# Output projection of the attention layer cut by rows of head batches and issued between the last heads; modulation products of layer 1 inside the earlier batches

## The chip, the cores and the metric

The kernel runs on one core of one Trainium2 chip. The metric is the device time of one execution in microseconds (us). TensorE (PE) multiplies, VectorE (DVE) and ScalarE (ACT) read its results out of PSUM and do the elementwise work, GpSimd (POOL) does a little elementwise work from SBUF, and SyncE (SP) issues nearly all DMAs, in program order on one queue. Each engine works off its own list in order and waits on semaphores.

## The reference

Two layers over 256 tokens of width 1024. Layer 0 mixes tokens by causal pooling, layer 1 by dilated attention; each is followed by a mixture of 64 experts. Every sublayer is scaled, shifted and gated by a condition vector c:

```python
mod = silu(c) @ ada_w[i] + ada_b[i]            # sh1, sc1, g1, sh2, sc2, g2
hm  = x * (1 + sc1) + sh1
y   = dilated_attention_mixer(hm, w_in, w_out) # layer 1: 16 heads, 3 groups of keys,
                                               # mixed heads @ w_out at its end
x   = layer_norm(ALPHA * x + (1 + g1) * y)
hf  = x * (1 + sc2) + sh2
x   = layer_norm(ALPHA * x + (1 + g2) * moe(hf))
```

All of it is f32. The change touches `mixed @ w_out` of layer 1 and the order of the `silu(c) @ ada_w` products.

## The kernel before, in words

**Modulation.** `ada_w` of both layers is cut in 24 pieces of 1024x512 (2 MB each), numbered n = 0 to 23. `load_ada(n)` is SP's DMA. `ada(n)` on PE is 8 products with c, packed four abreast into one PSUM bank (`part_bank`); ACT rounds the result to f32r (`ada(n)` there), DVE puts the lower part beside it (`lower_rows`), and when the next piece comes, `flush()` on PE adds bias and parts with two matmuls into bank 6 + n % 2 (`BSUM`), which ACT copies to `modb`. Pieces 12 to 23 belong to layer 1: 16 to 19 shift and scale of its expert sublayer, 20 and 21 the gate of attention, 22 and 23 the gate of the experts. Before the change 12 to 16 are done ahead of attention, 17 to 21 inside it (`ada_of_head`: 17, 18, 19 in batches 0, 1, 2, and 20 and 21 in the last), 22 and 23 behind it.

**Attention.** Keys, queries and values are projected from h in slices: slice n is 1 MB of `attn_w_in`, for a batch `hb` of four such heads, nine slices a batch; PSUM bank 6 + n % 2. Products are f32 by three f32r matmuls (`three`: high by high, low by high, high by low). So each slice is cast by ACT (`slice_high`, line 760) and its rest taken by DVE (`slice_low`, line 421) into one of two buffers `wr`. SP loads slice n into one of four units as soon as slice n - 4 has been lowered (`w_lo`), with the `load_ada`s written in between.
There are 16 heads of 64 columns; what the code counts as a head h, and this text too, is a pair of them for one tile of 128 of the queries, again 16 in all (`place`). For each: `scores(h)` on PE (line 1419), `head_scores` on DVE (bias, line 1088, and maximum, line 1093), exponential (line 792) and division (line 796) on ACT, eight transposes on PE (line 1443) to banks 2 and 3, copies to `pT` by ACT and DVE (lines 802, 1111), the product with the values on PE (line 1456) to bank 4, and DVE's copy to `mixedT` (line 1120), which signals `o_ready`. While the heads of batch hb run, the slices of batch hb + 1 are projected between them (`proj_of_head`: two per head, three in the last head of a batch). In the last batch nothing is left to project. There ACT and DVE also cast the mixed heads of the batches that are done (`mixed_high`, line 782, `mixed_low`, line 1099).

**Output projection.** Slices 36 to 39 are four column blocks of 256 of `attn_w_out`, each with all 1024 rows. A block needs all sixteen heads, so the four come after head 15: 192 matmuls of 256 columns. Slices 38 and 39 are cast while 36 and 37 are multiplied. Then PE does ada(22) and ada(23), and `norm(2)` on DVE and ACT adds, gates and normalizes (`residual`, lines 884 to 895; `deviation`; ACT's line 701), token tile 0 then 1; `modulate` makes h for the experts (POOL tile 0, DVE tile 1, lines 403 and 405). `moe(1)` begins with PE transposes (line 1182) and the router (line 1248), and its loop over 32 pairs of experts follows.
SP, behind head 15: the shared expert's weights, ada piece 22 once slice 39 is lowered, and the experts once `y_ready` and `ada_mm` 24 are there.

Of the kernel before, what the change touches and what calls it, by code (L numbers as in the profile page):

```python
# [131 lines left out]
def build(nc, a, out):  # L132
    ctx = ExitStack()
    with ctx:
# [118 lines left out]
        ada_unit = [0, 2, 4, 6, 4, 0, 2, 4, 0, 2, 6, 4, 0, 2, 6, 4, 9, 9, 9, 9, 9, 9, 2, 0]  # L253
# [5 lines left out]
        def part_bank(n):  # L259

            return 5 if n % 2 == 0 or 16 <= n < 22 else (3 if n == 15 else 4)
# [105 lines left out]
        def ada_of_head(hb, hh):  # L367

            return {(0, 1): 17, (1, 1): 18, (2, 1): 19, (3, 0): 20, (3, 2): 21}.get((hb, hh))
# [55 lines left out]
        def _(sp):  # L425
# [90 lines left out]

            def load_slice(n):
                if n < 9 * BATCHES:
                    src = a["attn_w_in"][n % 9, n // 9]
                else:  # L520
                    src = a["attn_w_out"][n - 9 * BATCHES]
                sp.dma_start(units(n % RAW, 1), src).then_inc(raw_in[n % RAW], 16)
# [9 lines left out]
            for n in range(RAW, SLICES):  # L532
                if n in (RAW, 20, 29, 38):
                    m = 17 + (RAW, 20, 29, 38).index(n)
                    sp.wait_ge(ada_mm, m)
                    load_ada(m)
                sp.wait_ge(w_lo, n - RAW + 1)
                load_slice(n)
            sp.wait_ge(ada_mm, 21)
            load_ada(21)  # L540
            sp.wait_ge(w_lo, SLICES - 2)
            load_ada(23)
            sp.wait_ge(ada_mm, 22)
            sp.wait_ge(o_ready, HEADS)
            shared(1)
            sp.wait_ge(w_lo, SLICES)
            load_ada(22)
            sp.wait_ge(y_ready, 3 * TT)
            sp.wait_ge(ada_mm, 24)
# [85 lines left out]
        def _(act):  # L635
# [150 lines left out]
            for hb in range(BATCHES):  # L786
                for hh in range(HB):
                    h = hb * HB + hh
                    before, after = proj_of_head(hb, hh)
                    for j in range(2):  # L790
                        act.wait_ge(max_ready, 2 * h + j + 1)
                        nc.scalar.activation(sp_[:, j], sp_[:, j], ACT.Exp, bias=negmax[:, j:j + 1],
                                             accum_out=zsum[:, j:j + 1]).then_inc(p_exp, 1)
# [9 lines left out]
                    if hb == BATCHES - 1 and hh < HB - 1:  # L803
                        mixed_high(hh)
                    for n in after:
                        projected(n)
            flush()
            act.wait_ge(o_ready, HEADS)
            mixed_high(BATCHES - 1)
            slice_high(SLICES - 2)  # L810
            slice_high(SLICES - 1)
            ada(22)
            norm(2, (0,))
            ada(23)
            norm(2, (1,))
            flush()
# [5 lines left out]
        def _(dve):  # L822
# [57 lines left out]
            def residual(n, t):  # L880

                gate = G1 if n % 2 == 0 else G2
                dve.wait_ge(y_ready, TT * n + t + 1)
                V.tensor_tensor(PS[:, 2 * t:2 * t + 2, :], PS[:, 2 * t:2 * t + 2, :],
                                modb[:, gate].rearrange("p (b n) -> p b n", b=2), ALU.mult).then_inc(y_read, 1)
                dve.wait_ge(y_read, TT * n + t + 1)
                step(V.scalar_tensor_tensor(tmp[:, t], x[:, t], ALPHA, PS[:, 2 * t:2 * t + 2, :].rearrange("p b n -> p (b n)"),
                                            ALU.mult, ALU.add))
# [14 lines left out]
            def norm(n):  # L903
# [6 lines left out]
                if n == 2:  # L910
                    lower_rows(22)
# [9 lines left out]
                if n == 2:  # L921
                    lower_rows(23)
# [179 lines left out]
            for h in range(HEADS):  # L1102
# [17 lines left out]
                last = copy(in_order(mixedT, 2 * hb + pair)[:, 2 * it:2 * it + 2], PS[:, 4, 0:P].rearrange("p (r i) -> p r i", r=2))  # L1120
# [3 lines left out]
                if hb == BATCHES - 1:  # L1124
                    mixed_low(hh)
                elif hh == HB - 1:
                    head_scores(h + 1)
            for n in (SLICES - 2, SLICES - 1):
                slice_low(n)
# [11 lines left out]
        def _(pe):  # L1141
# [259 lines left out]

            for n in range(9):
# [21 lines left out]
            for hb in range(BATCHES):  # L1424
                for hh in range(HB):
# [9 lines left out]
                    if n is not None and before:  # L1435
                        ada(n)
                    if h:
                        pe.wait_ge(pT_act, h)
                        pe.wait_ge(pT_dve, h)
                    for j in range(2):  # L1440
# [8 lines left out]
                    if h:  # L1449
                        pe.wait_ge(o_ready, h)  # L1450
                    _, pair, it = place(h)
                    for c in range(4):
                        for j in range(2):
                            col = (0, 1, it, it)[c] * BCOL + (2 * pair + j) * HD
                            v = qkv[:, hb % 2, (0, 0, 1, 2)[c], 2, col:col + HD]
                            last = mm(PS[j * HD:(j + 1) * HD, 4, 0:P], v, pT[:, j, c * P:(c + 1) * P], start=c == 0, stop=c == 3,  # L1456
# [5 lines left out]
            pe.wait_ge(hT_act, 12)  # L1462
            pe.wait_ge(hT_dve, 12)
            for n in range(SLICES - 4, SLICES):
                q = n - (SLICES - 4)
                pe.wait_ge(w_lo, n + 1)
                w = wr[:, n % 2]
                for t in range(TT):
                    for k in range(KD):
                        def parts(ph, pw):  # L1470
                            return (hThi, hTlo)[ph][:, k, t * P:(t + 1) * P], w[:, pw, k, :]
                        last = three(PS[:, 2 * t + q // 2, (q % 2) * BCOL:(q % 2 + 1) * BCOL], parts, k == 0, k == KD - 1)
                    if q == 3:
                        last.then_inc(y_ready, 1)
                if q < 3:
                    last.then_inc(proj_mm, 1)
            for n in (22, 23):
                ada(n)
            flush()
# [7 lines left out]
def packed(v):  # L1487
# [16 lines left out]
    v["attn_w_out"] = k_p(v["attn_w_out"][0], BCOL)  # L1504
# [21 lines left out]
```

## Time and profile before

| | us |
|---|---|
| median of 3 runs | 1578.89 |
| lowest, highest | 1572.59, 1582.16 |
| the profiled execution | 1582.94 |
| its span, first to last instruction | 1581.2 |

The profile is of one execution. Its times are us from the span's start. In a timeline a row is: start, duration, engine, line and operation, output and inputs, how many; in brackets the idle time of the engine just before and what ended it. In the chain of waits a row is: start, duration, what the end of the program hung on in that time. A row of a stretch gives the busy time of each engine with the number of instructions, then the granted TensorE clock (1.00 is 2.4 GHz, 0.50 is 1.2 GHz), the share of the DMA engines, and GB/s.

### The profile page before, as it was taken

Reading aid. Unit: us, or ns where it says so; the run is one execution under the profiler, and the core shown is the slowest. Engines: PE = TensorE matmul, PEld = TensorE weight load, DVE = VectorE, ACT = ScalarE, POOL = GpSimd, SP = SyncE. Lnnn points to the kernel's source line nnn. Section 1 sums busy time; section 2 is a strip of 40 time slices with the busy share of each in tenths; the row PEclk is TensorE's granted clock in tenths of the full one; section 3 lists DMA queues with packets and bytes.
Section 4 is the critical chain, followed back from the end, with each engine's and each line's share of the span. In section 5 each row is a group of like instructions: output and inputs, shape, how many; then the busy total and the mean of one; then the engine's idle time right before and its main releaser. Section 6 shows DMA issues by size and latency. Waiting matters only on the chain.

```text
span 1581.2 us, 19822 instructions
## 1 busy us (share of the span) xinstructions
PE 1477.7 (93%) x7858; PEld 873.9 (55%) x7858; DVE 500.6 (32%) x966; ACT 400.0 (25%) x633; POOL 98.6 (6%) x77
## 2 busy tenths in 40 slices
PE   4998999999999999959999997879999999999995
PEld 1454555455455454449899995745454454454552
DVE  2115222222222222254545545451222222222224
ACT  1123111121121111234545554231111111111112
POOL 1003022000000000051000000030200000000001
PEclk8998999999999999979999997879999999999997
DMA  9786599999999999555353543356999999999990
GB/s 377 317 363 288 239 398 423 426 427 425 427 427 423 424 424 423 233 228 201 131 206 109 211 183 137 141 240 250 419 426 423 428 426 425 425 424 425 420 393 27
DMA packets 50042, 520.23 MB, mean 329 GB/s; under 512 B 5752, under 2 KB 6008, under 8 KB 7880
## 3 DMA queue, kind: packets, MB, share of 16 engines
q1 hardware_dynamic: 48584, 514.73, 78.8%
q0 software_dynamic: 1408, 4.79, 0.9%
q8 instruction: 37, 0.61, 0.1%
q14 instruction: 13, 0.11, 0.0%
HBM read 518.44 MB, written 1.05 MB: 329 GB/s over the span
## 4 chain that ended last, share of the span: by engine, by line
PE 89%; DVE 5%; ACT 2%; DMA 2%; issue 1%; SPq 0%; DVEq 0%; ACTq 0%
PE psum L1336 28%; PE psum L1361 15%; PE psum L1292 8%; PE psum L1283 8%; PE psum L1380 5%; PE psum L1381 5%; PE psum L1382 5%; PE psum L1171 2%; DMA weights<-in_ada_w 2%; PE psum L1202 2%; PE psum L1256 2%; PE psum L1232 2%; PE psum L1443 1%; PE psum L1456 1%; PE psum L1274 1%
## 5 line engine op out<-in xcount | busy, mean ns | idle before, releaser
L1336 PE MATMUL psum<-weights,slots_of_tokens 128*64 128x512 f32 x2048 | 452.2, 592 | 0.0
L1336 PEld LDWEIGHTS psum<-weights,slots_of_tokens 128*64 128x64 f32 x2048 | 175.8, 137 | 263.8 <-issue 263.8
L1361 PE MATMUL psum<-weights,hidden_T 128*64 128x512 f32 x1024 | 233.8, 597 | 4.3
L1047 DVE SCALAR_TENSOR_TENSOR slot_rows<-psum,slot_weight,slot_rows 128x512 fp32r<-128x512 f32 x128 | 96.1, 751 | 243.7 <-ACT slot_rows L745 243.7
L1361 PEld LDWEIGHTS psum<-weights,hidden_T 128*64 128x64 f32 x1024 | 80.9, 136 | 128.5 <-issue 128.5
L1033 DVE TENSOR_TENSOR hidden<-gate,psum 128x256 f32<-128x256 f32 x64 | 27.0, 423 | 372.4 <-ACT gate L737 372.4
L1292 PE MATMUL psum<-slot_rows,slots_T 128*128 128x512 f32 x528 | 140.1, 407 | 3.7 <-DVE slot_rows L1047 3.7
L1283 PE MATMUL psum<-slot_matrix,h_parts 128*128 128x512 f32 x512 | 141.9, 399 | 0.0
L1292 PEld LDWEIGHTS psum<-slot_rows,slots_T 128*128 128x128 f32 x528 | 94.2, 188 | 74.5 <-issue 57.3
L737 ACT ACTIVATE gate<-psum 128x256 f32<-128x256 f32 x64 | 24.7, 386 | 409.7 <-PE psum L1336 409.7
L745 ACT ACTIVATE slot_rows<-psum,slot_weight 128x512 fp32r<-128x512 f32 x128 | 88.1, 689 | 156.6 <-PE psum L1361 156.6
L1380 PE MATMUL psum<-h_transposed_high,slice_parts 128*128 128x256 f32 x384 | 110.1, 287 | 5.2 <-DVE slice_parts L421 3.3
L421 DVE TENSOR_TENSOR slice_parts<-weights,slice_parts 128x2048 fp32r<-128x2048 f32 x38 | 88.9, 2347 | 69.1 <-ACT slice_parts L760 69.1
L1381 PE MATMUL psum<-h_transposed_low,slice_parts 128*128 128x256 f32 x384 | 108.6, 283 | 0.0
L1382 PE MATMUL psum<-h_transposed_high,slice_parts 128*128 128x256 f32 x384 | 108.6, 283 | 0.0
L1283 PEld LDWEIGHTS psum<-slot_matrix,h_parts 128*128 128x128 f32 x512 | 91.5, 189 | 16.8
L1035 DVE COPY slots_of_tokens<-psum 128x512 f32<-128x512 f32 x64 | 44.2, 691 | 136.2 <-PE psum L1283 136.2
L760 ACT CAST slice_parts<-weights 128x2048 fp32r<-128x2048 f32 x40 | 75.8, 1895 | 12.6 <-PE psum L1382 12.1
L1380 PEld LDWEIGHTS psum<-h_transposed_high,slice_parts 128*128 128x128 f32 x384 | 73.5, 192 | 8.3 <-issue 7.3
L1380 PE MATMUL psum<-slice_parts,h_transposed_high 128*128 128x256 f32 x256 | 74.0, 289 | 2.0 <-ACT h_transposed_high L782 2.0
L1381 PEld LDWEIGHTS psum<-h_transposed_low,slice_parts 128*128 128x128 f32 x384 | 73.6, 192 | 0.0
L1382 PEld LDWEIGHTS psum<-h_transposed_high,slice_parts 128*128 128x128 f32 x384 | 73.6, 192 | 0.0
(179 smaller groups left out, 1452.3 us busy)
## 6 DMA issues: line engine op xcount, KB each, us to landing
weights<-in_exp_w_gu SPq DMA_DIRECT2D x128, 2048.0 KB, 13.5
weights<-in_exp_w_down SPq DMA_DIRECT2D x128, 1024.0 KB, 11.6
weights<-in_ada_w SPq DMA_DIRECT2D x24, 2048.0 KB, 10.9
weights<-in_attn_w_in SPq DMA_DIRECT2D x36, 1024.0 KB, 4.8
weights<-in_pool_w_in SPq DMA_DIRECT2D x2, 2048.0 KB, 31.4
weights<-in_pool_w_out SPq DMA_DIRECT2D x1, 4096.0 KB, 13.2
weights<-in_sh_w_gu SPq DMA_DIRECT2D x2, 2048.0 KB, 10.8
weights<-in_attn_w_out SPq DMA_DIRECT2D x4, 1024.0 KB, 4.8
```

The costliest lines, as they stand in the source:

```text
L421: ops.tensor_tensor(wr[:, n % 2, 1], slice_w(n), wr[:, n % 2, 0].bitcast(F32), ALU.subtract).then_inc(w_lo, 1)
L745: nc.scalar.activation(yw[:, 0, half * HALF:(half + 1) * HALF], PS[:, BD + half, :], ACT.Copy, scale=wslot[:, 0:1]).then_inc(lo.yh, 1)
L760: copy(wr[:, n % 2, 0], slice_w(n)).then_inc(w_hi, 1)
L1035: copy(XgT[1 - i // 4][:, 2 * (i % 4), :], PS[:, BG, :]).then_inc(lo.copy_dve, 1)
L1047: V.scalar_tensor_tensor(yw[:, 1, c], PS[:, BD + half, :], wslot[:, 0:1], yw[:, 0, c].bitcast(F32), ALU.mult, ALU.subtract).then_inc(lo.yl, 1)
L1283: last = mm(PS[:, bank, :], hfs[:, s, t, k, :], Pm[b][:, t, :], start=s == 0 and t == 0, stop=s == 1 and t == TT - 1)
L1292: last = mm(PS[:, 2 * t + half, :], PT[:, t * P:(t + 1) * P], yw[:, s, half * HALF:(half + 1) * HALF], start=False, stop=True, skip_group_ ...
L1336: last = mm(PS[j * SLOTS:(j + 1) * SLOTS, BGU, :], XgT[ob][:, k, s0:s0 + SLOTS], gu_w(ws + j)[:, k, :], start=k == 0, stop=k == KD - 1, ti ...
L1361: last = mm(PS[j * SLOTS:(j + 1) * SLOTS, BD + half, :], HT[:, k, j * SLOTS:(j + 1) * SLOTS], dn_w(ws + j)[:, k, half * HALF:(half + 1) * ...
L1380: mm(out, *parts(0, 0), start=first, stop=False)
L1381: mm(out, *parts(1, 0), start=False, stop=False)
L1382: return mm(out, *parts(0, 1), start=False, stop=last)
```

## The change

Four things are changed together.

1. `attn_w_out` is cut by rows: slice 36 + q holds the 256 rows of `mixed` that head batch q produces, with all 1024 columns. `out_project(q)` multiplies them: 2 token tiles x 2 column halves x 2 row blocks x 3 = 24 matmuls of 512 columns, summed over q in PSUM (`mixer_bank`: banks 6, 7 for tile 0, banks 4, 5 for tile 1). q = 0, 1, 2 stand ahead of the transposes of heads 13, 14, 15; q = 3 behind head 15. `residual` reads the new banks.
2. ada pieces 17 to 23 all stand in batches 0 to 2 (PE, ACT and DVE), in partial bank 5; SP's loads of them move to `ADA_AT`. ACT and PE flush piece 23 at head 13.
3. The product with the values goes to bank 2 in place of 4, so PE now waits for the copy of head h - 1 (`o_ready`) ahead of the transposes of head h, not ahead of its value product.
4. `slice_high`/`slice_low` of 38 and 39 move into heads 13 and 14.

```diff
-        ada_unit = [0, 2, 4, 6, 4, 0, 2, 4, 0, 2, 6, 4, 0, 2, 6, 4, 9, 9, 9, 9, 9, 9, 2, 0]
+        ada_unit = [0, 2, 4, 6, 4, 0, 2, 4, 0, 2, 6, 4, 0, 2, 6, 4, 9, 9, 9, 9, 9, 9, 9, 9]
...
-            return {(0, 1): 17, (1, 1): 18, (2, 1): 19, (3, 0): 20, (3, 2): 21}.get((hb, hh))
+            return {(0, 1): 17, (0, 3): 18, (1, 1): 19, (1, 2): 20, (1, 3): 21, (2, 1): 22, (2, 3): 23}.get((hb, hh))
+        def mixer_bank(t):
+            return 6 - 2 * t
...
+            ADA_AT = (RAW, 15, 19, 23, 26, 28, 33)
-                if n in (RAW, 20, 29, 38):
-                    m = 17 + (RAW, 20, 29, 38).index(n)
+                if n in ADA_AT:
+                    m = 17 + ADA_AT.index(n)
                     sp.wait_ge(ada_mm, m)
                     load_ada(m)
                 sp.wait_ge(w_lo, n - RAW + 1)
                 load_slice(n)
-            sp.wait_ge(ada_mm, 21)
-            load_ada(21)
-            sp.wait_ge(w_lo, SLICES - 2)
-            load_ada(23)
-            sp.wait_ge(ada_mm, 22)
             sp.wait_ge(o_ready, HEADS)
             shared(1)
-            sp.wait_ge(w_lo, SLICES)
-            load_ada(22)
             sp.wait_ge(y_ready, 3 * TT)
-            sp.wait_ge(ada_mm, 24)
             experts(1)
...
+                    if h == HEADS - HB + 1:
+                        flush()
...
                     if hb == BATCHES - 1 and hh < HB - 1:
                         mixed_high(hh)
+                        if hh:
+                            slice_high(9 * BATCHES + hh + 1)
...
-            flush()
             act.wait_ge(o_ready, HEADS)
             mixed_high(BATCHES - 1)
-            slice_high(SLICES - 2)
-            slice_high(SLICES - 1)
-            ada(22)
-            norm(2, (0,))
-            ada(23)
-            norm(2, (1,))
-            flush()
+            norm(2)
...
-                last = copy(in_order(mixedT, 2 * hb + pair)[:, 2 * it:2 * it + 2], PS[:, 4, 0:P].rearrange("p (r i) -> p r i", r=2))
+                last = copy(in_order(mixedT, 2 * hb + pair)[:, 2 * it:2 * it + 2], PS[:, 2, 0:P].rearrange("p (r i) -> p r i", r=2))
...
                 if hb == BATCHES - 1:
                     mixed_low(hh)
+                    if hh in (1, 2):
+                        slice_low(9 * BATCHES + hh + 1)
...
-            for n in (SLICES - 2, SLICES - 1):
-                slice_low(n)
...
+            def out_project(q):
+                n = 9 * BATCHES + q
+                pe.wait_ge(w_lo, n + 1)
+                pe.wait_ge(hT_act, 8 + q + 1)
+                pe.wait_ge(hT_dve, 8 + q + 1)
+                w = wr[:, n % 2].rearrange("p w k n -> p w (k n)").rearrange("p w (k n) -> p w k n", k=2)
+                for t in range(TT):
+                    for half in range(2):
+                        for k in range(2):
+                            def parts(ph, pw):
+                                return (hThi, hTlo)[ph][:, 2 * q + k, t * P:(t + 1) * P], w[:, pw, k, half * HALF:(half + 1) * HALF]
+                            last = three(PS[:, mixer_bank(t) + half, :], parts, q == 0 and k == 0, q == BATCHES - 1 and k == 1)
+                    if q == BATCHES - 1:
+                        last.then_inc(y_ready, 1)
+                if q < BATCHES - 1:
+                    last.then_inc(proj_mm, 1)
...
+                    if hb == BATCHES - 1 and hh:
+                        if hh == 1:
+                            flush()
+                            pe.wait_ge(ada_mod, 24)
+                            pe.wait_ge(proj_copied, 9 * BATCHES)
+                        out_project(hh - 1)
                     if h:
                         pe.wait_ge(pT_act, h)
                         pe.wait_ge(pT_dve, h)
+                        pe.wait_ge(o_ready, h)
...
-                    if h:
-                        pe.wait_ge(o_ready, h)
...
-            for n in range(SLICES - 4, SLICES):
-                q = n - (SLICES - 4)
-                pe.wait_ge(w_lo, n + 1)
-                w = wr[:, n % 2]
-                for t in range(TT):
-                    for k in range(KD):
-                        def parts(ph, pw):
-                            return (hThi, hTlo)[ph][:, k, t * P:(t + 1) * P], w[:, pw, k, :]
-                        last = three(PS[:, 2 * t + q // 2, (q % 2) * BCOL:(q % 2 + 1) * BCOL], parts, k == 0, k == KD - 1)
-                    if q == 3:
-                        last.then_inc(y_ready, 1)
-                if q < 3:
-                    last.then_inc(proj_mm, 1)
-            for n in (22, 23):
-                ada(n)
-            flush()
+            out_project(BATCHES - 1)
             moe(1)
...
-    v["attn_w_out"] = k_p(v["attn_w_out"][0], BCOL)
+    v["attn_w_out"] = v["attn_w_out"][0].reshape(BATCHES, 2, P, D).transpose(0, 2, 1, 3).reshape(BATCHES, P, UNIT)
```

## Rows read from the trace of the kernel before

**Rows 1.** Page of the profile, busy time over the span: us, share, instructions.

```profile
PE 1477.7 (93%) x7858; PEld 873.9 (55%) x7858; DVE 500.6 (32%) x966; ACT 400.0 (25%) x633; POOL 98.6 (6%) x77
```

**Rows 2.** Busy time by stretch: inside the batches, and heads 14 and 15.

```profile
780.00:840.00 60.00, 58.37 (x520) 56.34 (x520) 33.51 (x46) 30.26 (x41) 0.00 (x0) 1.00 0.47 176
...
985.00:997.00 12.00, 6.33 (x49) 5.13 (x48) 6.04 (x15) 4.55 (x9) 0.00 (x0) 0.66 0.01 1
```

**Rows 3.** Timeline of PE, value products of heads 4 to 6 and ada between.

```profile
835.40 1.09 PE L1456 MATMUL psum<-probabilities_T,qkv 128*64 128x128 f32 x16
...
847.31 0.35 PE L1380 MATMUL psum<-h_transposed_high,slice_parts 128*128 128x256 f32 x1 [0.40 <-issue]
...
853.22 1.09 PE L1456 MATMUL psum<-probabilities_T,qkv 128*64 128x128 f32 x16
...
868.04 1.09 PE L1456 MATMUL psum<-probabilities_T,qkv 128*64 128x128 f32 x16
```

**Rows 4.** DMA issues between 690 and 1000 us: count, KB each, median us to landing.

```profile
weights<-in_ada_w SPq DMA_DIRECT2D x6, 2048.0 KB, 9.9
```

**Rows 5.** Chain of waits, heads 12 to 15.

```profile
967.65 1.95 PE psum L1443 x8
...
970.32 1.46 DVE scores L1088 x6
971.81 1.28 DVE negative_maximum L1093 x2
...
974.04 0.52 DVE h_transposed_low L1099
...
975.53 1.95 PE psum L1443 x8
...
991.74 1.96 PE psum L1443 x8
```

**Rows 6.** Timeline of PE, scores of head 14.

```profile
972.33 2.08 PE L1419 MATMUL psum<-qkv 64*128 64x256 f32 x12
```

**Rows 7.** Chain of waits, from the end of head 15 to the router.

```profile
996.49 0.73 PE psum L1159
...
998.27 0.52 ACT h_transposed_high L782
...
1000.16 0.21 PE psum L1381
...
1002.84 0.12 PE psum L1382
...
1012.77 1.92 ACT slice_parts L760
1014.71 2.30 DVE slice_parts L421
1017.03 7.69 DMA weights<-in_ada_w
...
1043.60 7.06 PE psum L1248 x32
```

**Rows 8.** Timeline of DVE, same stretch: fold, residual of tiles 0 and 1, modulation.

```profile
1016.92 0.68 DVE L393 TENSOR_TENSOR folded_shift<-norm_gain_bias,modulation 128x512 f32<-128x512 f32 x1
...
1021.45 1.23 DVE L884 TENSOR_TENSOR psum<-psum,modulation 128x1024 f32<-128x1024 f32 x1 [0.34 <-PE psum L1382]
...
1029.82 1.23 DVE L884 TENSOR_TENSOR psum<-psum,modulation 128x1024 f32<-128x1024 f32 x1
...
1038.03 1.23 DVE L405 TENSOR_TENSOR residual_or_h<-residual_or_h,modulation 128x1024 f32<-128x1024 f32 x1
```

**Rows 9.** Timeline of DVE, the norm between the layers: residual of tiles 0 and 1.

```profile
675.36 1.23 DVE L884 TENSOR_TENSOR psum<-psum,modulation 128x1024 f32<-128x1024 f32 x1 [0.37 <-DVE slot_of_token L1053]
...
680.15 1.23 DVE L884 TENSOR_TENSOR psum<-psum,modulation 128x1024 f32<-128x1024 f32 x1
```

**Rows 10.** Chain of waits in the expert loop: four f32r matmuls of 512 columns.

```profile
1090.39 0.93 PE psum L1283 x4
```

More of the change, by code:

```diff
@@ L259, in part_bank @@
         def part_bank(n):
-            return 5 if n % 2 == 0 or 16 <= n < 22 else (3 if n == 15 else 4)
+            return 5 if n % 2 == 0 or 16 <= n else (3 if n == 15 else 4)
         def ada_w(n):
@@ L882, in residual @@
                 gate = G1 if n % 2 == 0 else G2
+                b0 = mixer_bank(t) if n == 2 else 2 * t
+                y = PS[:, b0:b0 + 2, :]
                 dve.wait_ge(y_ready, TT * n + t + 1)
-                V.tensor_tensor(PS[:, 2 * t:2 * t + 2, :], PS[:, 2 * t:2 * t + 2, :],
-                                modb[:, gate].rearrange("p (b n) -> p b n", b=2), ALU.mult).then_inc(y_read, 1)
+                V.tensor_tensor(y, y, modb[:, gate].rearrange("p (b n) -> p b n", b=2), ALU.mult).then_inc(y_read, 1)
                 dve.wait_ge(y_read, TT * n + t + 1)
-                step(V.scalar_tensor_tensor(tmp[:, t], x[:, t], ALPHA, PS[:, 2 * t:2 * t + 2, :].rearrange("p b n -> p (b n)"),
-                                            ALU.mult, ALU.add))
+                step(V.scalar_tensor_tensor(tmp[:, t], x[:, t], ALPHA, y.rearrange("p b n -> p (b n)"), ALU.mult, ALU.add))
                 step.settle()
@@ L909, in norm @@
                 deviation(n, 0)
-                if n == 2:
-                    lower_rows(22)
                 if n == 0:
@@ L920, in norm @@
                     lower_rows(12)
-                if n == 2:
-                    lower_rows(23)
             def route(L):
@@ L1455, in _ @@
                             v = qkv[:, hb % 2, (0, 0, 1, 2)[c], 2, col:col + HD]
-                            last = mm(PS[j * HD:(j + 1) * HD, 4, 0:P], v, pT[:, j, c * P:(c + 1) * P], start=c == 0, stop=c == 3,
+                            last = mm(PS[j * HD:(j + 1) * HD, 2, 0:P], v, pT[:, j, c * P:(c + 1) * P], start=c == 0, stop=c == 3,
                                       tile_position=(0, j * HD))
@@ L1461, in _ @@
             flush()
-            pe.wait_ge(hT_act, 12)
-            pe.wait_ge(hT_dve, 12)
-            for n in range(SLICES - 4, SLICES):
-                q = n - (SLICES - 4)
-                pe.wait_ge(w_lo, n + 1)
-                w = wr[:, n % 2]
-                for t in range(TT):
-                    for k in range(KD):
-                        def parts(ph, pw):
-                            return (hThi, hTlo)[ph][:, k, t * P:(t + 1) * P], w[:, pw, k, :]
-                        last = three(PS[:, 2 * t + q // 2, (q % 2) * BCOL:(q % 2 + 1) * BCOL], parts, k == 0, k == KD - 1)
-                    if q == 3:
-                        last.then_inc(y_ready, 1)
-                if q < 3:
-                    last.then_inc(proj_mm, 1)
-            for n in (22, 23):
-                ada(n)
-            flush()
+            out_project(BATCHES - 1)
             moe(1)
```

## Prediction

> **What bounds the kernel now.** Look first at the page's busy times: PE is busy for 93% of the span [rows 1], so what counts is work added to or taken from PE, and the few places where PE stands idle. The busy times by stretch show where these are. Inside the batches PE works 58.4 of 60 us at 2.4 GHz, and the other engines half of that: each instruction added there is paid in full. In the last batch, with no slice left to project, PE works 6.3 of 12 us at a mean granted clock of 0.66 [rows 2]: there a chain of short steps through DVE, ACT and PE sets the time, so PE has room, but DVE and ACT have little. The chain of waits then shows the third place, the tail behind head 15: from the last value product (its end is where the first row of [rows 7] begins, 996.49) to the end of the modulation that lets PE transpose for the experts (1038.03 + 1.23 = 1039.26 [rows 8]) it takes **42.8 us**. The 192 matmuls of the projection, a DMA of piece 22 that holds the chain for 7.69 us once slice 39 is lowered [rows 7], ada(22) and ada(23) and the norm lie on it. The router follows at 1043.60 [rows 7]. From there on the change touches nothing, so I price three stretches: batches, last heads, tail.
>
> **Batches: four more ada.** Three ada stand in batches 0 to 2 before, seven after. Value product to value product, head 5 with an ada takes 853.22 - 835.40 = 17.82 us, head 6 with as many projections and none takes 14.82: an ada costs 3.0 us, of which 0.4 is PE waiting for ACT to free the sum's bank for the next projection of that parity [rows 3]. That wait comes only where the sum's number has the parity of the next slice: for 17, 18 and 19 before, for 17, 18, 20 and 21 after. So the four add 4 x 2.6 + 0.4 = **+10.8 us**. Nothing hides that, since PE is full [rows 2]. Their ACT and DVE parts (two copies, one subtraction, under 2 us a piece) fit beside engines that are half idle there. DMA: `load_ada` is now ahead of the slice load in six places and waits for the ada before it. An ada piece lands after 9.9 us [rows 4], and the slice queued behind it soon after, since the pair is moved together; I take 10 to 11 us from the end of the ada. The tightest places are slices 19 and 28, behind the ada of a batch's last head: their cast could begin when transposes and one more slice are done, 1.0 + 5.8 + ACT's copy 0.6, with the 0.4 and the sum's matmuls 0.6, 8.4 us after the ada. So the cast (1.92) comes 1.6 to 2.6 us late; DVE meanwhile is at the value copy and the lower part of the slice before, 2.30 [rows 7], so 0 to 1.5 us come through at each of two places; I take 0. If the landing were still later, head scores of the next batch would wait behind that slice on DVE, and the head's transposes on PE for them. The new wait for `o_ready` ahead of the transposes stands behind a whole slice of projection, 48 matmuls at 0.12 [rows 7] or 5.8 us, in which DVE only needs its copy: free here.
>
> **Last heads.** I lay out time from the start of head 12's transposes (967.65). Before: heads 13 and 15 begin their transposes at 7.88 and 24.09 [rows 5], and head 15's value product ends at 28.84 [rows 7]. The same chain after the change:
> - Head 12: transposes 1.95 and copy to 2.7, bias to 4.15, maxima to 5.4 [rows 5]. PE's value product ends at 4.75 (as 991.74 to 996.49 for head 15 [rows 5, 7]), scores of head 14 take 2.08 [rows 6], to 6.8. Now the new wait: ACT stands at `flush()` ahead of head 13's exponential until PE has done the two sum matmuls (0.73 + 0.44), then copies for 0.6, so piece 23 is in `modb` at 8.65 (the same three steps run from 996.49 to 998.27 [rows 7]). Only then come exponential, reciprocal and division for head 13, about 2.6 us; they end near 11.3, still beside out_project(0).
> - **out_project**: 24 matmuls of 512 columns. Four cost 0.93 at 2.4 GHz [rows 10], so 5.6 us. At 1.2 GHz a matmul of 256 columns takes 0.21 against 0.12 [rows 7], so one of 512 about 0.43 (an estimate from these), 10.3 us for all 24. PE has been working for some 6 us when q = 0 starts at 8.7, and in the tail of before the clock rose 3 us after the first projection matmul, near 1002.7 [rows 7]; so I give q = 0 6.5 us. Head 13's transposes begin at 15.2, not 7.88.
> - Heads 14 and 15: the period is transposes 1.0 (half of the 1.95 at the low clock), copy 0.75, bias 1.46, maxima 1.28 [rows 5], value copy 0.3 (part of the 0.95 between the end of head 13's maxima and the start of its lower part; ada's `lower_rows`, now gone from there, is the rest), `mixed_low` 0.52 [rows 5], signals 0.15, out_project 5.6: 11.1 us. out_project must wait for `mixed_low` of the same batch of channels, which stands behind `head_scores` on DVE; that wait is the new link. The casts of slices 38 and 39 (ACT 1.92, DVE 2.30 us [rows 7]) delay the reciprocal, and so put division's end at 8.8 us of the period, 2.3 us ahead of out_project's end: hidden now, but only by it. Before, the three periods were 7.88, and 16.21 for two [rows 5], with ada(21) in the path of one.
> - Between value product and out_project(2) PE idles 2.4 us, as no scores are left. I take the clock as falling there and add 1.5 us (7 matmuls at the low price). Nearest row: [rows 2] for 985 to 997, at 0.66.
> So head 15's transposes begin at 15.2 + 11.1 + 11.1 + 1.5 = 38.9, and its value product ends 3.0 later, at 42.0, not 28.84: **+13.2 us**. Bounds: +11.7 with the clock high throughout; each out_project at the low clock would add 4.7, so +25 at worst.
>
> A rule of the Trainium skill bears on this. The rows show the last heads at 0.66 of full clock [rows 2], with eight transposes at 1.95 us [rows 5]. The page "TensorE: Matmul & The Clock Gate", section "HAM oscillation — how this bites in real kernels", says that bursts of matmuls between waits keep falling back to the low clock and pay the ramp each time, and its Part 4 says that transposes do not count as busy. By that rule each of the three projections between heads would start low, as in my second rival; by the rows the clock had risen to full within the tail of before.
>
> **Tail.** From the end of head 15's value product: DVE's copy 0.5 with its signal, then cast on ACT, lower part on DVE and PE's start, 1.4 us (998.27 for the cast, and the projection's matmul at 1000.16 is its third, 0.4 to 0.5 us behind the first [rows 7]): PE starts at 1.95, DVE is free at 1.85. Tile 0 takes 12 matmuls: 2.8 us at the high clock, 5.2 at the low, 4.2 with a rise on the way, so `y_ready` comes at 6.2. DVE needs 1016.92 to 1021.11 = 4.2 us for `fold_norm` [rows 8], which used to lie beside the projection; it ends at 6.05. Residual of tile 0 starts at 6.25. Without ada(22) in ACT's way the second tile's starts 4.8 us later, as in the norm between the layers [rows 9] (before: 8.4, from 1021.45 to 1029.82 [rows 8]). From there to the end of the modulation it took 9.44 us (1029.82 to 1039.26 [rows 8]), which I keep, since `lower_rows`, which goes, stood in the shadow of ACT. Sum 6.25 + 4.8 + 9.4 = 20.5, against 42.8: **-22.3 us**. With `y_ready` at the extremes (4.8 with fold in front, 7.2) it is -22.5 to -21.3. Next in line behind it are ACT's two casts for the experts, then the router 4.3 us after the modulation, as before [rows 7, 8]. The loads of router and shared weights start at the end of head 15 in both; the router's has 24.8 us in place of 47.1 (20.5 or 42.8, and 4.3), and 0.25 MB lands well within that beside 3 MB of shared weights, by the 9.9 us of a 2 MB piece [rows 4]. The experts' loads still start ahead of the router.
>
> **Sum.** +10.8 + 13.2 - 22.3 = **+1.7 us**: the span 1581.2 becomes 1582.9, the execution 1582.94 becomes 1584.6. That execution lies 4.05 above the median of the runs, 1578.89, so the median after should be **1580.6 us**. The work taken from the tail is nearly all still paid: the 23 us of projection matmuls are issued between heads whose chain they lengthen, and ada 22 and 23, with 20 and 21 which lay in idle time, go where PE is full.
>
> **Rivals.**
> - *Faster, the projection fits the gaps.* If the products slip beside DVE's and ACT's work, the heads keep their old 8 us periods plus the flush, +3 in place of +13.2: total -8.5, 1570.4. For it: PE is idle half of that stretch [rows 2]. Against it: program order puts out_project between scores and transposes, and it waits for `mixed_low`, so it cannot use the idle time before. It decides if out_project starts before the maxima end.
> - *Slower, the clock stays low between heads.* Every out_project at the low price: 3 x 4.7 less the 2.4 already counted, and 1 us for tile 0 in the tail, +13: total +14.5, 1593.4. It decides if the rows of out_project lie 0.43 us apart beyond the first 3 us. For it: 0.66 in [rows 2], and the skill's rule. Against: PE will be busy 9 of 11 us per head.
> - *Slower, slices late.* The loads behind `load_ada` block ACT and through it DVE: if the pairs land 3 us later than I take, two boundaries and one head pay about 2 us each, +6: 1586.6.
> - *The overlap isn't there.* If something keeps q = 1 and 2 behind head 15 (a flush, `w_lo` 39), two pieces of 5.6 return to the tail, and the heads lose 2 x 3; total +7, 1585.9.
>
> **How the numbers follow.** Forecast, between -3 and +5 around the sum: 0.58. Fits the gaps or is otherwise clearly faster: 0.17. Clock: 0.10. Slices late: 0.09. No overlap: 0.06. The runs of before spread by 0.6%, so a 1% change, 15.8 us, is about what can be told from none. Faster by over 1% would need the first rival and the ada hidden as well: 0.05. Slower by over 1% is the clock rival with some slices late: 0.07. The range takes the first rival and most of the clock rival: 1569 to 1593.
>
> **What would show it.** Heads 5 and others with an ada again at 17.8, and 7 of them. In heads 14 and 15 a period near 11, with DVE's `h_transposed_low` (line 1099 before) as what releases the first matmul of out_project; exponential of head 13 released by ACT's own `modulation` copy. The tail from last value product to the modulation's end at 20 to 21 us, with no DMA in the chain. Wrong if the period is 8 to 9 or above 13, if granted clock in the last heads stays under 0.7, or if PE waits at the start of a batch for a slice's lower part more than it does now.

## The result, and the profile after

The changed kernel takes **1581.62 us** (median of 20 runs, 1576.69 to 1589.05) against 1578.03 us for the kernel before (20 runs, 1572.59 to 1585.31): ratio 1.003, 95% interval 1.0018 to 1.0041. That is 3.6 us slower in the medians, forecast were 1.7, a change of 0.3%, far below the 2% from which one calls a kernel slower. Its profiled execution took 1582.43 us and has a span of 1580.7 us.

To see where time went I cut each trace at five points that both kernels have: the start of head 0's value product, the start of head 12's transposes, the end of head 15's value product, the end of `modulate` of tile 1, and the first matmul of the expert loop. Each number is a difference of row starts or ends in the timelines of PE and DVE, in us; "to expert loop" runs from the end of `modulate` to the first matmul of the loop:

| profile | batches | last heads | tail | to expert loop | sum |
|---|---|---|---|---|---|
| before | 201.8 | 28.8 | 42.8 | 42.0 | 315.4 |
| before, second | 201.9 | 26.5 | 43.1 | 42.7 | 314.1 |
| before, third | 201.8 | 28.8 | 42.7 | 42.0 | 315.3 |
| changed | 215.5 | 40.8 | 20.9 | 37.1 | 314.2 |
| changed, second | 215.3 | 41.0 | 21.3 | 37.1 | 314.6 |
| changed, third | 215.1 | 40.8 | 20.9 | 37.1 | 313.9 |
| e1 slices first | 212.4 | 40.8 | 20.9 | 37.1 | 311.1 |
| e2 ada only | 215.5 | 26.5 | 40.9 | 42.4 | 325.2 |
| e3 project behind | 215.3 | 30.0 | 35.3 | 37.1 | 317.6 |
| e4 flush at 12 | 215.4 | 40.5 | 22.4 | 40.1 | 318.4 |
| e5 ada at 12 | 212.6 | 40.4 | 20.8 | 40.4 | 314.3 |
| e6 transposes first | 215.2 | 33.9 | 20.9 | 42.2 | 312.2 |
| e7 combined | 209.8 | 32.1 | 20.9 | 37.1 | 299.9 |

Changed against before: **+13.7, +12.0, -21.9, -4.9**. The first three are the forecast's +10.8, +13.2 and -22.3. The fourth was not forecast. Head 0's value product itself starts anywhere from 761.2 to 766.4 us in these six profiles of the two kernels, so some 5 us of difference between executions arise ahead of everything that the change touches.

**Batches.** The timeline of PE in the changed kernel, value products of heads 4 and 5, the ada of head 6, and a slice:

```profile
840.00 1.09 PE L1470 MATMUL psum<-probabilities_T,qkv 128*64 128x128 f32 x16
...
857.18 1.09 PE L1470 MATMUL psum<-probabilities_T,qkv 128*64 128x128 f32 x16
...
865.23 1.92 PE L1162 MATMUL psum<-weights,condition_repeated 128*32 128x512 f32 x16
...
870.26 0.36 PE L1371 MATMUL psum<-slice_parts,h_transposed_high 128*128 128x256 f32 x1 [1.58 <-issue]
```

Head 5 now takes 857.18 - 840.00 = 17.18 us against 17.82 in [rows 3]: the wait of 0.4 is absent, as the prediction's rule of parity says (it comes only where the number of the sum and of the next slice are both even or both odd, and so share a bank). The other 0.24 means that an ada without the wait costs 2.4 us here and not 2.6. But in head 6 PE waits 1.58 us where 0.4 was due. ACT's timeline (the idle time before each cast, and its releaser) shows why:

```profile
824.09 1.90 ACT L758 CAST slice_parts<-weights 128x2048 fp32r<-128x2048 f32 x1 [1.87 <-DMA weights<-in_attn_w_in]
...
861.23 1.91 ACT L758 CAST slice_parts<-weights 128x2048 fp32r<-128x2048 f32 x1 [3.35 <-DMA weights<-in_attn_w_in]
...
901.37 1.90 ACT L758 CAST slice_parts<-weights 128x2048 fp32r<-128x2048 f32 x1 [1.97 <-DMA weights<-in_attn_w_in]
```

Slices 19, 23 and 28 come late. SP had issued their ada pieces at 813.72, 850.03 and 890.90; the casts start 10.4, 11.2 and 10.5 us later. Behind slices 19 and 28 PE waits at the first transposes of the next batch, 0.77 and 0.87 us, for ACT's division.

**Last heads.** Chain of waits of the changed kernel (start, duration, what the end hung on):

```profile
981.83 1.95 PE psum L1459 x8
...
986.62 2.01 PE psum L1428 x12
988.63 0.72 PE psum L1150
989.35 0.32 PE psum L1151
989.70 0.60 ACT modulation L648
990.35 0.50 PE psum L1371
...
996.11 0.89 PE psum L1459 x8
...
999.19 1.28 DVE negative_maximum L1084 x2
...
1000.77 0.53 DVE h_transposed_low L1090
...
1001.43 0.47 PE psum L1371
...
1012.49 0.47 PE psum L1371
...
1013.43 0.43 PE psum L1371
...
1017.06 0.23 PE psum L1371
...
1019.81 0.89 PE psum L1459 x8
```

Read it against [rows 5]: head 13's transposes no longer wait for ACT's division but stand behind out_project(0), which stands behind scores, the two sum matmuls (lines 1150, 1151) and ACT's copy of the sum (line 648). In heads 14 and 15 `mixed_low` (line 1090) releases out_project (line 1371), and out_project releases the transposes. The period is 11.05 us, then 12.65. In out_project(2) the first three matmuls lie 0.23 to 0.31 us apart, the next eight 0.40 to 0.43, the rest 0.23: the clock fell just behind its start, not ahead of it. Granted clock by stretch:

```profile
985.00:997.00 12.00, 11.29 (x62) 8.69 (x58) 3.21 (x10) 3.34 (x7) 0.00 (x0) 0.82 0.00 1
997.00:1009.00 12.00, 8.93 (x62) 7.27 (x64) 7.43 (x15) 6.68 (x11) 0.00 (x0) 1.00 0.00 0
1009.00:1020.00 11.00, 8.52 (x44) 6.80 (x45) 5.57 (x12) 4.82 (x8) 0.00 (x0) 0.84 0.01 2
```

PE is busy 28.7 of 35 us, at 0.82 to 1.00, where [rows 2] had 6.3 of 12 at 0.66.

**Tail.** Chain of waits and, last, the router: fold's first step, residual of tile 0 and of tile 1, the modulation's end, transposes, router.

```profile
1024.37 0.70 DVE folded_shift L397
...
1028.64 1.25 DVE psum L881
...
1033.51 1.16 DVE psum L881
...
1042.28 1.24 DVE residual_or_h L409
1043.56 3.47 PE psum L1173 x15
...
1047.86 3.76 PE psum L1239 x32
```

No DMA and no ada is left there. DVE's fold of 4.2 us, which lay beside the projection in [rows 8], now decides when the residual starts. The router takes 3.76 us, not the 7.06 of [rows 7]: it is at the high clock from its first matmul. That is where the 4.9 us of the last stretch come from (3.3 here, the rest in the matmuls behind it). Granted clock of the changed kernel in the 15 transposes and in the router, then of the kernel before in the router:

```profile
1043.56:1047.03 3.47, 3.47 (x15) 3.06 (x15) 0.69 (x1) 3.40 (x4) 3.40 (x3) 0.50 0.97 413
1047.86:1051.61 3.75, 3.75 (x33) 3.75 (x34) 0.00 (x0) 0.24 (x1) 3.44 (x2) 1.00 1.04 446
```

```profile
1043.60:1050.66 7.06, 7.06 (x33) 7.06 (x34) 0.00 (x0) 0.68 (x1) 3.45 (x2) 0.50 1.00 427
```

In the changed kernel the clock rises between the transposes and the router; in the kernel before, with the same transposes ahead of the router, it is low to the router's end.

### The profile page after: what moved, and what is told of

Its sections match the earlier page's. It is cut to its first block, busy times and chain, and to the rows that moved or that the text cites. A ratio compares the mean times of both kernels' runs of the same rounds, so it can differ in the third digit from the quotient of the medians.

```text
span 1580.7 us, 19647 instructions
## 1 busy us (share of the span) xinstructions
PE 1467.6 (93%) x7762; PEld 861.8 (55%) x7762; DVE 501.0 (32%) x966; ACT 399.4 (25%) x633; POOL 98.2 (6%) x77
## 4 chain that ended last, share of the span: by engine, by line
PE 88%; DVE 6%; DMA 3%; ACT 2%; issue 1%; SPq 0%; DVEq 0%; ACTq 0%
PE psum L1327 28%; PE psum L1352 15%; PE psum L1283 8%; PE psum L1274 8%; PE psum L1371 4%; PE psum L1372 4%; PE psum L1373 4%; PE psum L1162 2%; PE psum L1193 2%; PE psum L1247 2%; PE psum L1223 2%; DMA weights<-in_ada_w 1%; DMA weights<-in_attn_w_in 1%; PE psum L1265 1%; PE psum L1459 1%
## 5 line engine op out<-in xcount | busy, mean ns | idle before, releaser
L1371 PE MATMUL psum<-slice_parts,h_transposed_high 128*128 128x256 f32 (+1 forms) x224 | 68.6, 306 | 8.6 <-DVE h_transposed_low L1090 5.5
## 6 DMA issues: line engine op xcount, KB each, us to landing
weights<-in_exp_w_down SPq DMA_DIRECT2D x128, 1024.0 KB, 11.2
weights<-in_sh_w_gu SPq DMA_DIRECT2D x2, 2048.0 KB, 10.8
```

The source lines that it names most:

```text
L1371: mm(out, *parts(0, 0), start=first, stop=False)
```

## The experiments

e1 to e4 ran on one chip, e5 to e8 on another; each was also timed against the kernel before. The changed kernel itself ran beside e5 to e8 only. Stretches are those of the one profiled execution of each, and executions of one kernel differ by several us, so the medians of 5 to 12 runs are given too.

**e1_slices_first.** Are the 2.9 us that the batches cost above the forecast the late slices?

```diff
-            ADA_AT = (RAW, 15, 19, 23, 26, 28, 33)
+            ADA_AT = (RAW, 16, 20, 24, 27, 29, 34)
```

> The changed kernel, with each of SP's loads of an ada piece issued one slice later, so that slices 15, 19, 23, 26, 28 and 33 go ahead of the piece and no longer wait for the ada before it. Theory (slices late): ACT's casts no longer wait for a DMA (7.7 us in the changed kernel), the three heads behind slices 19, 23 and 28 lose 0.9, 1.2 and 1.0 us, and the four extra ada cost 10.8 us as forecast, not 13.7: 3 us less than the changed kernel, ratio to the kernel before about 1.001. Rival (the waits are covered, the extra is something else, such as ACT's or DVE's queue): casts start earlier and the stretch from head 0's value product to head 12's transposes stays at 215.5 us.

Measured: batches 212.4, 3.1 less than changed, all else equal to 0.1 us; 1578.67 us, ratio 1.0005 (0.9996 to 1.0013). Group of ACT's casts from 780 us to head 12, first in the changed kernel, then in e1 (count | busy, mean | idle before, releaser):

```profile
L758 ACT CAST slice_parts<-weights 128x2048 fp32r<-128x2048 f32 x24 | 45.5, 1894 | 7.2 <-DMA weights<-in_attn_w_in 7.2
```

```profile
L758 ACT CAST slice_parts<-weights 128x2048 fp32r<-128x2048 f32 x24 | 45.4, 1891 | 0.0
```

The waits for a DMA are gone and with them the 3 us; the rival falls. What is left of the batches' cost, 212.4 - 201.8 = 10.6 us, is the forecast's 10.8 for four ada.

**e2_ada_only.** What does the move of the ada pieces do by itself?

```diff
 # the kernel before, with only:
-        ... 9, 9, 9, 9, 9, 9, 2, 0]
+        ... 9, 9, 9, 9, 9, 9, 9, 9]
-            return {(0, 1): 17, (1, 1): 18, (2, 1): 19, (3, 0): 20, (3, 2): 21}.get((hb, hh))
+            return {(0, 1): 17, (0, 3): 18, (1, 1): 19, (1, 2): 20, (1, 3): 21, (2, 1): 22, (2, 3): 23}.get((hb, hh))
 # SP's loads and waits and the partial bank as in the change; ada(22), ada(23) and their parts gone from the tail
```

> The kernel before with part 2 of the change alone: ada pieces 17 to 23 in batches 0 to 2, SP's loads as in the change; projection in column blocks behind head 15 and value product in bank 4 as before. Theory: the batches cost +13.7 us as in the changed kernel, the last heads lose ada 20 and 21 (-1.3), the tail loses only what ada 22 and 23 held up beyond the projection (42.8 to about 39.2): +8.8 us against before, ratio 1.0055. Rival (the two ada of the tail and the DMA ahead of them were the main cost there): the tail shrinks by 10 us or more and the kernel is level with before or faster.

Measured: batches +13.7, heads -2.4, tail -1.9, together +9.4 of the expected +8.8; 1592.35 us, ratio 1.0068 (1.0047 to 1.009). Two of its nine runs took 1580.2 and 1580.6, at a granted clock of 0.968 against 0.961 to 0.964 in the others; no profile shows one of them. The 2.4 us of the heads cannot be put down to ada 20 and 21: the second profile of the kernel before has the same 26.5 with both in place. The tail's chain in e2: the projection's first and last matmul, the residual.

```profile
1011.26 0.55 PE psum L1364
...
1033.90 0.13 PE psum L1366
1034.16 1.24 DVE psum L872
```

With the two ada and their DMA gone the tail still takes 40.9 us, since the projection lies on it from 1011.26 to 1034.03. The rival, a tail 10 us shorter, falls: the ada of the tail were nearly free there, the four more in the batches are not.

**e3_project_behind.** Is it worth anything to issue the products between heads?

```diff
-                        out_project(hh - 1)
...
-            out_project(BATCHES - 1)
+            for q in range(BATCHES):
+                out_project(q)
 # slice_high / slice_low of 38 and 39 behind head 15's casts
```

> The changed kernel with all four products by rows issued behind head 15 (slices 38 and 39 cast there too), the rest as changed. Theory (the products between heads cost 12 us there, but save some 17 us of the tail and the clock's ramp): heads 13 to 15 go back to periods near 8 us, from head 12's transposes to head 15's last value product 32 us instead of 40.8, the tail goes from 20.9 to 38.4: +8.7 us against the changed kernel, ratio to before 1.008. Rival (moving them is worth nothing, all is paid between the heads): within 2 us of the changed kernel, 1.003.

Measured: heads 30.0, tail 35.3, 3.5 us more than changed in both together (expected 8.7; the rival allowed 2). Median 1584.88, ratio 1.0032 (1.0017 to 1.0048). Chain of waits: transposes of heads 13, 14, 15, the last cast, the fold, the residual.

```profile
992.27 1.91 PE psum L1458 x8
...
999.72 1.19 PE psum L1458 x8
...
1006.45 1.96 PE psum L1458 x8
...
1023.19 1.92 ACT slice_parts L758
...
1027.35 0.70 DVE folded_shift L397
...
1031.62 1.24 DVE psum L881
```

Without the products between them heads 14 and 15 come in 7.45 and 6.73 us. So the three products lengthen the heads by 10.8 us (40.8 - 30.0) and shorten the tail by 14.4 (35.3 - 20.9). About three quarters of what is saved behind is paid in front. Neither theory's number was right; the truth lay between them. The three products take 17.2 us of the tail (1011.17 to 1028.38), and it grows by only 14.4: the first of them starts at once, while out_project(3) of the changed kernel waits 1.94 us for `mixed_low`, and DVE's fold ends 1.1 us behind out_project(3)'s first tile there and 0.3 us in e3.

**e4_flush_12.** Is the sum of piece 23 in head 13 a cost of its own?

```diff
 # ACT and PE
-                    if h == HEADS - HB + 1:          (PE: if hh == 1, ahead of out_project)
+                    if h == HEADS - HB:              (PE: ahead of scores(h + 1))
                         flush()
```

> The changed kernel with the sum of piece 23 at head 12, where PE and ACT stand idle, and not at head 13. Theory (the flush is a wait of its own in head 13): out_project(0) starts right behind the scores of head 14, 1.7 us earlier, and the exponential of head 13 3.5 us earlier; the heads are 1.7 us shorter, ratio to before 1.002. Rival (head 13 is bound by mixed_low and the clock's rise, so the flush is hidden): under 0.5 us.

Measured: out_project(0) starts right behind the scores, and head 13's transposes come 12.7 us behind head 12's, not 14.1. But heads and tail together are 62.8 us, 1.2 more than changed, and the median is 1584.82, ratio 1.0038 (1.0025 to 1.0051). Chain of waits, out_project(2), out_project(3) and the residual:

```profile
1010.15 0.77 PE psum L1371
...
1015.61 0.39 PE psum L1371
...
1023.29 0.76 PE psum L1371
...
1028.89 1.24 DVE psum L881
```

The 1.4 us are there and are lost again: out_project(2) now runs its first 13 matmuls at the low clock, and out_project(3) its first 14, with them its whole first tile, 5.5 us, so that `y_ready` is late where DVE's fold had covered it. The step that I expected happened, its worth did not arrive. That the earlier product is what moved the clock is argued from one profile: in the second profile of the changed kernel out_project(3) starts with six matmuls at the low clock too, and the intervals of the two kernels overlap.

**e5_ada_12.** Does an ada cost its price only where PE is full?

```diff
-... (2, 1): 22, (2, 3): 23}.get((hb, hh))
+... (2, 1): 22, (3, 0): 23}.get((hb, hh))
```

> The changed kernel with ada piece 23 at head 12, where PE idles 5.7 us, in place of batch 2. Theory (an ada costs its 2.6 to 3.0 us only where PE is full): from head 0's value product to head 12's transposes 2.6 us less, heads the same within 0.3, ratio 1.001. Rival (the price of an ada in the batches comes from ACT and DVE): less than 1 us saved, or given back in head 13, whose sum waits for the lower rows: ratio 1.003.

Measured: batches 212.6, 2.9 us less, heads 0.4 less: the theory's 2.6 to 3.0. Its last stretch was 40.4 against 37.1 us, as the clock fell again inside the router (4.75 us); median 1581.47, ratio 1.0022 (1.0006 to 1.0038), which cannot be told from the 1581.57 of the changed kernel beside it.

**e6_transposes_first.** Is the 11 us period order, or work?

```diff
 # PE: out_project from ahead of the transposes to behind them; flush at head 12
                     last.then_inc(t_mm, 1)
+                    if hb == BATCHES - 1 and hh:
+                        ...
+                        out_project(hh - 1)
 # DVE, last batch
+                if hb == BATCHES - 1:
+                    if hh >= 2:
+                        slice_low(9 * BATCHES + hh)
+                    if hh < HB - 1:
+                        inverse(h + 1)            # the reciprocal, ahead of the value copy
                 dve.wait_ge(o_mm, h + 1)
 # ACT: slice_high(9 * BATCHES + hh) behind the pT copies of heads 14 and 15
```

> The changed kernel with out_project(q) between the transposes and the value product of its head, the reciprocal of the next head ahead of DVE's copy, slices 38 and 39 cast one head later, and the sum of piece 23 at head 12. Theory (the period of 11.1 us is PE's out_project waiting for mixed_low, with the transposes behind it): PE's own work, 1.0 + 5.6 + 1.1 + 1.1, sets a period near 9, from head 12's transposes to the last value product 33.5 to 35 us instead of 40.8, at least 6 us off, ratio 0.999. Rival (DVE's and ACT's queues bind, with the casts): periods stay at 10.5 or more, 1 us off at most, ratio 1.002.

Measured: heads 33.9 us, 6.9 less; 1579.33 us, ratio 0.9996 (0.9979 to 1.0013), 2.2 us less than the changed kernel beside it. The rest went at the router: it ran at the low clock, and the last stretch took 42.2 us, 5.1 more. Chain of waits:

```profile
986.01 1.94 PE psum L1463 x8
987.95 0.43 PE psum L1379
...
996.64 1.04 PE psum L1463 x8
...
1001.16 2.20 DVE slice_parts L425
1003.36 0.09 DVE softmax_inverse L1095
...
1004.86 1.07 PE psum L1463 x8
```

Head 15 comes 8.3 us behind head 14, head 14 10.6 behind 13, as out_project(0) still starts with six matmuls at the low clock. What ends the shorter period is again a cast: slice 38's lower part (line 425) holds the reciprocal. The rival falls: one period is above its 10.5, but for the clock, and it allowed 1 us off in all. The sum of piece 23 at head 12 is in this kernel too, worth 1.4 us to head 13 in e4; the other moves of e6 were not tried one by one.

**e7_combined.** e1, e5 and e6 together, the sum of piece 23 behind head 14's scores.

> Slices ahead of the ada pieces, piece 23 at head 12 with its sum behind the scores of head 14, and transposes ahead of out_project, all in the changed kernel. Theory: the parts add, batches -3.1 - 2.6, heads -6.7, tail unchanged: 12 us less than the changed kernel in the stretches up to the router, ratio to the kernel before 0.995, and 0.998 at worst where the clock is low. Rival (what is taken out returns as time at the low clock): under half of it, ratio 0.999 or more.

Measured: batches -5.7 (expected -5.7), heads -8.7 (-6.7), tail equal, 14.4 us less than changed up to the router; 1572.04 us (1562.55 to 1576.28), ratio to before **0.9957** (0.9939 to 0.9975). In the medians it is 9.5 us faster than the changed kernel beside it and 6.4 faster than the kernel before, and the rival (0.999 or more) falls. But the profiled execution, 1562.68 us at a granted clock of 0.975, is one of two such; the ten others took 1570.3 to 1576.3 at 0.965 to 0.968, and no profile shows where their 7.6 us or more go. So the 14.4 us are this kernel at its best. In that execution the clock is at full from 978.5 us to past the last head:

```profile
971.00:978.50 7.50, 6.27 (x38) 4.87 (x39) 5.04 (x13) 4.94 (x11) 0.00 (x0) 0.60 0.01 2
978.50:990.00 11.50, 11.48 (x76) 9.42 (x77) 6.04 (x17) 6.50 (x13) 0.00 (x0) 1.00 0.00 0
990.00:1003.00 13.00, 12.30 (x82) 9.82 (x80) 8.02 (x11) 6.59 (x9) 0.00 (x0) 1.00 0.01 2
```

**e8_changed_again, e9_before_again, e10_before_third, e11_changed_third.** Both kernels unaltered, more profiles, to see which differences are of the kernel and which of the execution.

> The changed kernel, unaltered, on the same chip as the kernels beside it. Theory (between head 12 and the experts PE's clock falls and rises at places that differ from execution to execution): the stretches of the batches come out as before within 0.5 us (215.5), while heads, tail and router stage differ by up to 5 us from the first profile's 40.8, 20.9 and 37.1 us. Rival (the clock's course is the kernel's own): all four stretches the same within 0.3 us. Ratio 1.003 in both.

> The kernel before, unaltered, one more profile. Theory (the stage from the end of the modulation to the expert loop falls at 37 or at 42 us with PE's clock, in either kernel, from execution to execution): one of the two profiles of the kernel before in this call has it at 37 to 40, so that the 4.9 us by which the changed kernel's first profile was shorter there is no effect of the change. Rival (the longer wait ahead of the router in the kernel before fixes the clock's course): 42.0 within 0.3 in both, and 37.1 in the changed kernel.

> The kernel before, unaltered, a third profile; theory and rival as for the second: 37 to 40 us in one of the two, or 42.0 in both, from modulation to expert loop. Batches 201.8, heads 28.8, tail 42.8 us within 0.5 in both theories.

> The changed kernel, unaltered, a third profile. Theory: batches 215.4, heads 40.9, tail 21 us within 0.5, the stage behind them anywhere from 37 to 42. Rival: that stage at 37.1 within 0.3, as in both profiles of it so far.

Measured: the first six rows of the table; e8 1581.57 us, ratio 1.0018 (0.9999 to 1.0038); e9, e10 and e11 one execution each, 1577.84, 1582.70 and 1576.72. In e9 the clock did differ in the last heads (transposes of heads 13 and 14 in 1.20 and 1.19 us, heads 2.4 us shorter):

```profile
978.37 1.19 PE psum L1443 x8
...
1037.63 7.06 PE psum L1248 x32
```

But the stage to the expert loop was 42.0, 42.7 and 42.0 in the kernel before and 37.1 three times in the changed one, so there my theory does not hold: in profiled executions the router runs low in the one and high in the other. The rivals' margin of 0.3 us was missed by little in the tail of e8 (0.4 longer) and in the last stretch of e9 (0.7).

## Why the prediction was right

**Batches: right, one term set too low.** Forecast +10.8, measured +13.7. The four ada cost what [rows 3] gave (10.6 with the late slices taken out by e1, and e5 takes one back for 2.9). The term "0 to 1.5 us come through at each of two places; I take 0" is the one that failed: it was 3.1 us at three places. I had looked at slices 19 and 28 and let slice 23 go, behind an ada of a head in mid-batch. ACT waits 3.35 us there for the DMA, its copy of the sum that PE makes beside ada 20 comes late, and PE waits 1.58 us for the bank. The landing itself was as assumed, 10 to 11 us behind the ada. This is the effect of the rival "slices late" at half its price, but not on its condition: the pairs did not land 3 us later, one place more was hit.

**Last heads: right.** Forecast +13.2, measured +12.0. Head 13's transposes 14.1 us behind head 12's (15.2 forecast: out_project(0) took 5.8 us, not 6.5, as the clock was up when it began), then 11.05 (11.1), then 12.65 (12.6 with the 1.5 us for the low clock in out_project(2); the size was right, though the clock fell behind its third matmul and not in the idle time ahead of it). The link named, `mixed_low` to out_project, is the releaser in both heads. e3 confirms the price from the other side, e6 that much of it is the order and not the work.

**Tail: right.** Forecast -22.3, measured -21.9. Residual of tile 0 began 6.0 us behind the last value product (6.25), tile 1's 4.8 later, modulation 10.1 after that (9.4 forecast; the shift on DVE took 1.59 us in place of 0.93).

**Behind the tail: missed.** "From there on the change touches nothing" held for the work, not for the clock. The kernel before enters the router at 1.2 GHz and the changed one at 2.4, in three profiles each, 4.9 us in favour of the change. Why the clock is up by then, after a longer idle stretch of PE (9.47 us ahead of its first transpose against 5.48 ahead of the last sum in the kernel before), is not shown by any run. e2 and e6 have the low router at 7.06 us, e1, e3 and e7 the high one, and in e4 and e5 the clock falls again inside it (5.11 and 4.75 us).

**The sum.** The four stretches give -1.2 us in the profiles, without the router's clock +3.7, and the medians differ by +3.6. That these two agree proves nothing, since the gain at the router is in all three profiles. The three profiled executions of each kernel do not show the difference of the medians (1582.94, 1577.84, 1582.70 before against 1582.43, 1579.89, 1576.72). It does not hang on the slowest runs either: 4 of the changed kernel's 20 lie at 1586.6 to 1589.1 (2 of e8's 12 at 1588.3 to 1589.4) and none so high in the kernel before, but the other 16 still have a median of 1581.3. Those slowest runs have a granted clock of 0.963 to 0.966, the others of this kernel 0.967 to 0.972; no profile caught one of them, and which stretch is longer in them stays open. On e8's chip the difference is not clear of noise (0.9999 to 1.0038). So the three priced stretches came out as the mechanism says, +3.8 against +1.7, while the median at 1581.62, 1.0 us from the forecast's 1580.6, is in part luck: the forecast missed the router's 4.9 us, and something that no profile shows makes up for them in the medians.

**The rivals.** "Fits the gaps" does not hold in this order of instructions; e6 shows that it nearly holds in another. "The clock stays low" did not happen in the changed kernel, but e4 shows it at work for 13 matmuls of one product and 14 of the next. The Trainium skill's rule on bursts between waits ("TensorE: Matmul & The Clock Gate", section "HAM oscillation — how this bites in real kernels") shows in one product of three between the heads here: out_project(0) and (1) ran at 0.23 us a matmul, and out_project(2), behind 2.5 us of idle PE, fell to 0.43 after its third and was back at 0.23 from its twelfth. The prediction had read the rule as all three beginning low; none did. The other half of the rule in the prediction, that transposes do not count, has a case against it: between 1030.28 us and the router at 1047.86 PE of the changed kernel did transposes alone, and the clock rose there from 0.50 to 1.00. "The overlap isn't there" is excluded by the chain.

## What to carry to other kernels

Work taken out of a tail is only gained to the extent that its new place is idle: the ada pieces went from nearly free places to a full PE (e2, +9.4 us in its profile), the products into a chain whose period they lengthened (three quarters of the gain back). When an engine has idle time in a chain of short steps, put the filler behind the instruction that starts the chain's next step, not ahead of it, and keep casts for later work out of the way of the reciprocal: the same instructions gave 40.8 us in one order and 33.9 in another, though 5.1 of the 6.9 us were lost again at the router's clock. When a DMA with a wait of its own is put into a queue, count the slices behind it at every place, also where the wait seems early.

## What was not expected of the hardware

Time saved ahead of a clock change may come back as time at the low clock. In e4's profile head 13 came 1.4 us sooner, and the last two products ran 27 matmuls 0.43 us or more apart in place of the changed kernel's 8 at 0.40 to 0.43. One profile of e4 does not show that the one caused the other. The 32 small router matmuls took 7.06 us in all three profiles of the kernel before and 3.76 in all three of the changed one (3.75 in one), with nothing changed in them. In the changed kernel the clock rose behind 15 transposes, with nothing else on PE; in the kernel before it had not risen behind the same 15.
